# Local attention: the gate from VectorE to GpSimd, by way of a ScalarE copy, and the next group's rounded keys and queries from ScalarE to GpSimd

## The reference

```python
def windowed_sink_attention(q, k, v, sink, slopes):     # 16 heads, 4 key heads, width 64
    ...                                                 # each block of 128 queries sees 3 blocks of keys
    sc = jnp.einsum('bnqkgd,bnskd->bnkgqs', qb, kb).astype(jnp.float32) * scale + bias
    sc = jnp.where(valid[None, :, None, None], sc, -jnp.inf)
    m = jnp.maximum(jnp.max(sc, axis=-1, keepdims=True), sink_l)
    p = jnp.exp(sc - m)
    denom = jnp.sum(p, axis=-1, keepdims=True) + jnp.exp(sink_l - m)
    o = jnp.einsum('bnkgqs,bnskd->bnqkgd', (p / denom).astype(v.dtype), vb)
...
    return (oc * jax.nn.silu(gc)) @ w_out
```

## Time and profile before

| what | value |
|---|---|
| median of 3 runs | 2405.64 us (2405.22 to 2407.04) |
| the profiled execution | 2409.29 us, span 2408.0 us |
| TensorE matmul busy | 96% of the span |
| VectorE, ScalarE, GpSimd busy | 58%, 47%, 39% |
| local attention in the span | from about 1055 to 1232 us |

### The profile page before, as it was taken

How to read it: one execution, slowest core, us unless ns; L and a number is a source line. 1 busy time by engine, 2 the same in 40 slices (tenths; PEclk the granted TensorE clock), 3 DMA queues, 4 the chain that set the end, 5 groups by cost and what they waited for, 6 DMA issues and landing times.

```text
span 2408.0 us, 31494 instructions
## 1 busy us (share of the span) xinstructions
PE 2321.7 (96%) x12074; PEld 1925.0 (80%) x12074; DVE 1395.4 (58%) x1899; ACT 1133.0 (47%) x1796; POOL 929.6 (39%) x711
## 2 busy tenths in 40 slices
PE   5999999999999999999999999999999999999998
PEld 5888789878888888876678868788877888888887
DVE  6255599768884320139973743332776666666665
ACT  5322388778883221249952474232333333333334
POOL 1111256447642212335521122112265555555551
PEclk9999999999999999999999999999999999999999
DMA  8255300010003221100031221121211111111111
GB/s 307 76 158 168 93 6 1 4 34 1 1 1 123 87 74 44 53 1 1 10 106 44 77 79 44 36 96 53 71 35 53 53 53 53 53 53 53 53 53 70
DMA packets 154091, 146.48 MB, mean 61 GB/s; under 512 B 12295, under 2 KB 141365, under 8 KB 152021
## 3 DMA queue, kind: packets, MB, share of 16 engines
q1 hardware_dynamic: 153940, 144.45, 19.3%
HBM read 123.85 MB, written 16.78 MB: 58 GB/s over the span
## 4 chain that ended last, share of the span: by engine, by line
PE 81%; ACT 6%; DVE 5%; issue 5%; POOL 2%; DMA 1%; SPq 0%; ACTq 0%; DVEq 0%; POOLq 0%
PE ps L256 36%; PE ps L2650 15%; PE ps L2667 9%; PE ps L1126 5%; PE ps L1149 4%; PE ps L1136 4%; ACT C_PR L1807 1%; PE ps L1696 1%; DMA MKW<-in_ada_w 1%; POOL WSL L2567 1%; ACT B_PR L1210 1%; PE ps L1675 1%; PE ps L2626 1%; ACT B_PTH L1204 1%; PE ps L1662 1%
## 5 line engine op out<-in xcount | busy, mean ns | idle before, releaser
L243 POOL TENSOR_TENSOR WL<-WR,WH 128x1024 fp32r<-128x1024 f32 (+2 forms) x87 | 203.6, 2341 | 766.1 <-ACT WH L238 765.9
L256 PE MATMUL ps<-HH,WH 128*128 128x512 f32 (+2 forms) x1136 | 358.8, 397 | 0.0
L256 PE MATMUL ps<-HL,WH 128*128 128x512 f32 (+2 forms) x1136 | 352.1, 391 | 0.0
L256 PE MATMUL ps<-HH,WL 128*128 128x512 f32 x1104 | 341.3, 391 | 0.0
L256 PEld LDWEIGHTS ps<-HL,WH 128*128 128x128 f32 (+2 forms) x1136 | 212.4, 187 | 47.8
L256 PEld LDWEIGHTS ps<-HH,WH 128*128 128x128 f32 (+2 forms) x1136 | 208.3, 187 | 46.7 <-issue 4.1
L256 PEld LDWEIGHTS ps<-HH,WL 128*128 128x128 f32 x1104 | 208.2, 189 | 44.0
L2880 DVE TENSOR_TENSOR XF<-ps,XF 128x1024 f32<-128x1024 f32 x168 | 201.5, 1220 | 32.7 <-PE ps L2667 26.1
L2650 PE MATMUL ps<-HC,WSH 128*128 128x512 f32 x640 | 197.0, 389 | 0.0
L1162 DVE TENSOR_REDUCE NM<-ps 128x1 f32<-128x1024 f32 x128 | 156.5, 1223 | 33.5 <-PE ps L1126 32.0
L2567 POOL TENSOR_TENSOR WSL<-WSR,WSH 128x512 fp32r<-128x512 f32 x100 | 131.5, 1315 | 107.6 <-ACT WSH L2561 107.6
(11 more groups left out here) (433 smaller groups left out, 5183.0 us busy)
## 6 DMA issues: line engine op xcount, KB each, us to landing
WS<-in_w_ffn_in SPq DMA_DIRECT2D x44, 512.0 KB, 5.0
MKW<-in_ada_w SPq DMA_DIRECT2D x32, 512.0 KB, 4.3
spill<-X SPq DMA_DIRECT2D x3, 4096.0 KB, 13.6
OW<-in_w_ffn_out SPq DMA_DIRECT2D x22, 512.0 KB, 3.5
WR<-in_odd_w_in SPq DMA_DIRECT2D x19, 512.0 KB, 4.0
WR<-in_w_in SPq DMA_DIRECT2D x19, 512.0 KB, 3.9
WR<-in_even_w_in SPq DMA_DIRECT2D x17, 512.0 KB, 4.2
AWK<-in_ada_w SPq DMA_DIRECT2D x8, 1024.0 KB, 9.4
```

The lines of the kernel that those rows point to most:

```text
L243: pool.tensor_tensor(low[:, :, :], raw[:, :, :], high[:, :, :].bitcast(F32), ALU.subtract).then_inc(*w_low.up(t))
L256: last = pe.matmul(ps[0:w.out, 2 * s + h, :], wt[:, k, :], x[:, k, halves(h)], start=(k == 0 and n == 0), stop=(k == w.kt - 1 and n == len ...
```

## The change

The gate leaves VectorE. ScalarE copies the spread inverse sums from PSUM into C_G, in the odd unit 2g + 3, and GpSimd multiplies C_G in place by the silu gates in unit 2g + 4. TensorE's spread waits for ScalarE's copy of the group before, where it waited for VectorE's gate. The rounded keys and queries of the next head group are made by GpSimd as copies into the rounded format, in the same units (5, 7 and 9) in which ScalarE made them. Those of the first head group stay with ScalarE.

```diff
@@ pe_c_spread(g)
         if g:
-            pe.wait_ge(*c_gated.at(g - 1))
+            pe.wait_ge(*c_ri_moved.at(g - 1))
@@ VectorE
-    def dve_c_gate(g):
-        i, n = g // TT, g % TT
-        dve.wait_ge(*c_spread.at(g))
-        if g >= 2:
-            dve.wait_ge(*c_mixed.at(g - 2))
-        dve.tensor_tensor(C_G[:, g % 2, :].rearrange("p (t n) -> p t n", t=2),
-                          ps[:, 7, 0:2 * P].rearrange("p (t n) -> p t n", t=2), mix_pair(i, n),
-                          ALU.mult).then_inc(*c_gated.up(g))
...
-            if u % 2 == 0 and 4 <= u < NU + 4:
-                dve_c_gate((u - 4) // 2)
@@ ScalarE
+    def act_c_move_inverse(g):
+        act.wait_ge(*c_spread.at(g))
+        if g >= 2:
+            act.wait_ge(*c_mixed.at(g - 2))
+        act.activation(C_G[:, g % 2, :], ps[:, 7, 0:2 * P], ACT.Copy).then_inc(*c_ri_moved.up(g))
...
-            i = u // 16 + 1
-            if i < C_KV:
-                if u % 16 == 5:
-                    act_c_keys(i)
-                elif u % 16 in (7, 9):
-                    act_c_query(2 * i + (u % 16 - 7) // 2)
-            elif u % 16 == 5 and u < NU:
+            if u % 2 == 1 and 3 <= u < NU + 3:
+                act_c_move_inverse((u - 3) // 2)
+            if u == 16 * (C_KV - 1) + 5:
                 act_high(ODD_OUT[0])
@@ GpSimd
+    def pool_c_next_keys(i):
+        base = (i % 2) * HD
+        for r in range(2):
+            c_pool_in_turn()
+            pool.tensor_copy(C_KH[rows(r, HD), i, :], KC[base:base + HD, i // 2, :]).then_inc(*c_next_key.up(i, r))
+
+    def pool_c_next_query(t):
+        if t >= 4:
+            pool.wait_ge(*c_scored.at(2 * (8 * (t // 2 - 2) + 7) + t % 2, 1))
+        c_pool_in_turn()
+        pool.tensor_copy(C_QH[t % 4][:, :], QC[:, t, :]).then_inc(*c_next_query.up(t))
+
+    def pool_c_gate(g):
+        i, n = g // TT, g % TT
+        pool.wait_ge(*c_ri_moved.at(g))
+        c_pool_in_turn()
+        wide = C_G[:, g % 2, :].rearrange("p (t n) -> p t n", t=2)
+        pool.tensor_tensor(wide, wide, mix_pair(i, n), ALU.mult).then_inc(*c_gated.up(g))
...
             if u % 2 == 0 and 2 <= u <= NU:
                 pool_c_wide((u - 2) // 2)
+            if u % 2 == 0 and 4 <= u < NU + 4:
+                pool_c_gate((u - 4) // 2)
             if u % 2 == 1 and 5 <= u < NU + 5:
                 pool_c_mix((u - 5) // 2)
             i = u // 16 + 1
             if i < C_KV:
                 if u % 16 in (1, 2, 3, 4):
                     pool_c_bias(i, u % 16 - 1)
+                elif u % 16 == 5:
+                    pool_c_next_keys(i)
                 elif u % 16 == 6:
                     pool_c_keys(i)
+                elif u % 16 in (7, 9):
+                    pool_c_next_query(2 * i + (u % 16 - 7) // 2)
                 elif u % 16 in (8, 10):
                     pool_c_query(2 * i + (u % 16 - 8) // 2)
```

More of the change, by code:

```diff
@@ L1540, in evict @@
                 if i == 12:
-                    act_c_keys(0)
+                    act_c_keys()
                 elif i < 15:
@@ L1625, in build @@
     c_scored, c_turned, c_spread, c_summed = signal("c_scored"), signal("c_turned"), signal("c_spread"), signal("c_summed")
[L1626 to L1629, removed]
+    c_biased, c_low, c_inverse, c_added, c_key_low0, c_query_low0, c_sinks = signal("c_dve").steps(
+        "biased", "low", "inverse", "added", "key_low0", "query_low0", "sinks")
+    c_raised, c_high, c_moved, c_ri_moved, c_key_high, c_query_high, c_sink = signal("c_act").steps(
+        "raised", "high", "moved", "ri_moved", "key_high", "query_high", "sink")
     c_pool = signal("c_pool")
-    c_mixed, c_wide, c_bias, c_v_high, c_values, c_key_low, c_query_low = c_pool.steps(
-        "mixed", "wide", "bias", "v_high", "values", "key_low", "query_low")
+    c_mixed, c_gated, c_wide, c_bias, c_v_high, c_values, c_next_key, c_next_query, c_key_low, c_query_low = c_pool.steps(
+        "mixed", "gated", "wide", "bias", "v_high", "values", "next_key", "next_query", "key_low", "query_low")
     def window(n):
@@ L1776, in dve_attention_c, with act_c_keys @@
                 dve_c_low(u - 2)
-            if u % 2 == 0 and 4 <= u < NU + 4:
-                dve_c_gate((u - 4) // 2)
             if u % 2 == 1 and 5 <= u < NU + 5:
                 dve_c_add((u - 5) // 2)
-    def act_c_keys(i):
-        base = (i % 2) * HD
+    def act_c_keys():
         for r in range(2):
-            act.activation(C_KH[rows(r, HD), i, :], KC[base:base + HD, i // 2, :], ACT.Copy).then_inc(*c_key_high.up(i, r))
+            act.activation(C_KH[rows(r, HD), 0, :], KC[0:HD, 0, :], ACT.Copy).then_inc(*c_key_high.up(0, r))
     def act_c_query(t):
[L1788 to L1791, removed]
+        act.wait_ge(*vc_turned.at(1))
         act.activation(C_QH[t % 4][:, :], QC[:, t, :], ACT.Copy).then_inc(*c_query_high.up(t))
@@ L1862, in pool_c_keys @@
         for r in range(2):
-            pool.wait_ge(*c_key_high.at(i, 1))
             c_pool_in_turn()
@@ L1866, in pool_c_keys @@
                                C_KH[base:base + HD, i, :].bitcast(F32), ALU.subtract).then_inc(*c_key_low.up(i, r))
+    def pool_c_next_keys(i):
[14 more added lines that the diff above has]
+        pool.tensor_tensor(wide, wide, mix_pair(i, n), ALU.mult).then_inc(*c_gated.up(g))
     def pool_c_query(t):
-        pool.wait_ge(*c_query_high.at(t))
         c_pool_in_turn()
```

## The result

The changed kernel takes 2414.61 us (median of 5 runs, 2412.84 to 2415.83), the kernel before 2405.22 in the same comparison (median of 5, 2399.75 to 2407.04). The ratio is 1.0045, 95% interval 1.0034 to 1.0056: slower by 0.45%, some 9 to 11 us. The forecast was 2419.3, with a range of 2404 to 2424.

What follows compares the result with a forecast made beforehand. TensorE, VectorE and ScalarE were taken to share the bound of local attention within a few per cent. Backlog +10.1 and clock +3.6 us gave +13.7 on the median 2405.64: 2419.3 us, range 2404 to 2424.

Steps and rivals of the forecast that it cites:

- likeliest case: Local attention: GpSimd's backlog plus one to three clock falls, +11.9 to +15.5 us; chance 0.45.
- rival D: Local attention: GpSimd's backlog as worked out but no fall of the clock, +10.1 us, 2415.7; chance 0.24.
- +10.1 us for the backlog: GpSimd's late widenings delay TensorE's spread in the first three head groups: +3.1, +3.5 and +3.5 us.
- what is regained is at most TensorE's idle 0.18 us in the next group: After a late spread, TensorE can recover only its 0.18 us of shown idle time per group.
- +3.6 us for the clock: TensorE's clock halves after two of three stalls of about 3.5 us, costing 1.8 us each.
- The gate is worth nothing on VectorE: Taking VectorE's 32 gate multiplies away saves 0 us, since they lie under the loop TensorE - VectorE - ScalarE.
- ScalarE's copy at no cost: ScalarE's 32 copies of the spread inverse sums out of PSUM cost 0 while the spread is on time; uncovered, 10 us.
- ScalarE's relief, 5.1 us: Losing 6 key and 6 query roundings alone gives back 1.7 us in each of three head groups.
- Rival A: VectorE bounds local attention, so removing its gate and ScalarE's roundings saves 16.6 us, 2389; chance 0.06.
- B: Rival: GpSimd's backlog is absorbed and ScalarE's relief counts, -5.1 us, 2400.5; chance 0.06.
- C: Rival: GpSimd's copies near their lower bound and no clock falls, +2.6 us, 2408; chance 0.11.
- F: Rival: GpSimd's copies at their upper bound, +16 us more, 2435, or GpSimd and VectorE hinder each other; chance 0.08.

Runs made afterwards that it cites:

- e5: The kernel before with only GpSimd's two low parts of the next keys moved from unit 6 to unit 7; ratio to before 1.0040, stage +9.4 us.
- e4: The change with the gate left on VectorE and GpSimd's key and query roundings spread one piece per unit; ratio to before 0.9974, stage 156.1 us.
- e6: The whole change, gate and roundings on GpSimd, with the roundings spread out in e4's order; ratio to before 0.9989, stage 160.1 us.
- e7: e6 with the widening placed ahead of the mix in GpSimd's list; ratio to before 0.9978, stage 156.4 us.
- e9: The change with 14 unused filler matmuls on TensorE in the long stall of each of three head groups; ratio to before 1.0024, stage 169.7 us.
- e2: The change with the gate left on VectorE, so only the key and query roundings move to GpSimd; ratio to before 1.0032, stage 166.5 us.
- e3: The kernel before with VectorE's gate cut to 4 of 128 columns of each half from the third group on; ratio to before 0.9998.
- e10: e4 with VectorE's gate cut as in e3; ratio to the kernel before 0.9978, stage 155.8 us.
- e1: The change with the next keys and queries still rounded by ScalarE, so only the gate moves; ratio to before 1.0008, stage +2.4 us.

## Why the prediction was right, point by point

The median grew by 9.4 us where 13.7 were forecast. 2414.61 lies in the stated range, but just below the 2415 to 2422 of the likeliest case and nearer to rival D (2415.7), which had no fall of the clock. The falls came all the same; the backlog was smaller than worked out. So the direction and the mechanism were right, both terms were mis-sized, and that the time lies near D's is chance.

- **Where the loss is.** The spread waits for GpSimd's widening, once for 3.5 us in each of three head groups. That was the forecast's main step, and the change's trace shows it with the length that was worked out (about 3.5; measured 3.62, 3.49, 3.49). e5 shows that the place in the list is enough, e4, e6 and e7 that the same work spread out in the list costs no more than 2.7 us of waits (e7) or 8.4 in short pieces (e6), and leaves the stage shorter than before.
- **The durations on GpSimd.** Taken from the nearest rows, they held: key copy 1036 ns, query copy of 128 partitions 1036 (forecast 1.04 for both), gate 731 to 736 (forecast as the mix, 738). The list from the first mix to the fifth widening's end took 1129.41 - 1101.30 = 28.1 us, forecast 28.75. The table groups took the 10.32 us worked out. The difference lies behind them, in the 0.16 us that I put behind every operation: ahead of the copies and the low parts it was less, 0.06 to 0.13 us, as between the mix at 1121.04 and the copy at 1121.90.
- **+10.1 us for the backlog was too much.** e9, which has no falls behind its stalls, gives it alone: 169.7 - 162.6 = 7.1 us (7.4 without the first group), 0.2 of them in the fourth head group. Two steps failed by size. In the second head group of e9 the fifth spread came 3.2 us later, counted from the first, than before, not 3.7: the list was shorter. And "what is regained is at most TensorE's idle 0.18 us in the next group" didn't hold: from that spread to the next head group's first, e9 took 19.29 us against 19.92, so 0.6 us came back over four groups. There it made two spreads 4.79 us apart where before had 5.44. Together 2.6 us, where I had 3.5. Idle time that a row shows ahead of an instruction isn't all the slack: when the other engines are ahead, the matmuls' own starts close up too.
- **+3.6 us for the clock.** Measured 3.1 (3.3 without the first group), by other parts than I put it: three falls at 0.5 to 1.8 us, not two at 1.8, since two of them were half as long. That the totals lie so close is partly luck. The granted clock after the first and the third stall was

```profile
1076.00:1080.00 4.00, 1.95 (x9) 1.18 (x10) 0.62 (x3) 0.93 (x2) 3.55 (x5) 0.74 0.01 2
1080.00:1084.00 4.00, 4.00 (x23) 3.21 (x24) 2.42 (x6) 2.60 (x6) 3.50 (x4) 0.84 0.00 0
```

```profile
1169.00:1173.00 4.00, 2.93 (x13) 2.17 (x14) 0.95 (x3) 0.67 (x2) 3.62 (x4) 0.63 0.01 4
1173.00:1177.00 4.00, 4.00 (x26) 2.95 (x26) 2.42 (x8) 3.00 (x9) 3.34 (x6) 0.94 0.01 2
```

  that is (0.26 + 0.16) x 4 / 0.5 = 3.4 us at 1.2 GHz, and 3.4 again, against 6.9 after the second by the rows of the change shown with e9. In this execution the trace is with the rule of the Trainium skill that I had weighed ("TensorE: Matmul & The Clock Gate", part 1): a fall after each of the three. The stalls of 2.5 us in e2 and e5 were followed by a fall in four of six cases, the waits of up to 1.08 us in e6 by none.
- **The gate is worth nothing on VectorE.** e3 (-0.2 us) and e10 (-0.3) confirm it, with VectorE's waits for the scores up by 6.7 us in e3.
- **ScalarE's copy at no cost.** Nearly: 378 ns each. It costs 0.3 us in the fourth head group, nearly all in the group in which ScalarE rounds a weight tile, and 2.1 us over the other three where ScalarE keeps its roundings (e1).
- **ScalarE's relief, 5.1 us.** Seen in e4: 1.7 and 1.9 us in the second and third head group, as forecast (1.7 each), and 1.6 in the first without its first group. 5.1 in all.
- **Sum.** 7.1 + 3.1 = 10.2 of the stage's 10.3 us, forecast 13.7; without the first group 7.4 + 3.3 = 10.7, all of it. Rival A is out by e3, B by the spread's waits, C by the copies' 1036 ns and by e9, D by the falls, F by the same 1036 ns. F's other part, GpSimd and VectorE hindering each other, is not seen in this stage: GpSimd's mix took 738 ns before and after, VectorE's bias 610 and 611, its low part 954 both times.

## What to carry to other kernels

An engine at half load can still be the bound. What counts is what stands in its list ahead of a small result that a full engine waits for: add up the list from the last point at which it waited, and compare it with the time at which the result is due. Relief of an engine pays only where no other loop is equally long; cut the operation to a few columns and see. Put long side work behind the urgent operation, one piece in each slot: the same work went from +0.45% (the change) to -0.22% (e7) that way.

## What the runs showed of the hardware that was not expected

- A stall of about 3.5 us in a stage that is otherwise busy brought TensorE to 1.2 GHz each time, but for 3.4 or for 6.9 us, so the same stall cost 0.5 to 0.7, 1.8 and 0.9 us beside what it held up itself. One of 2.5 us did so in four of six cases. Filling the stall with matmuls that nobody reads held the clock.
- A matmul of the 32-bit identity with itself (128x128, not rounded) is two records of the trace: 26 took 5.97 us, 0.23 us each. A transpose of the same size is one: six are six records, and took 0.88 us.
- GpSimd's rounding copy takes 1036 ns for 1024 columns, the same on 64 and on 128 partitions.
- One execution can carry a wait and a fall of the clock that the next doesn't. The wait of 2.91 us and the fall behind it are nearly all of the 6.1 us by which the changed kernel entered the stage earlier. The VectorE operation waited for took 3.27 us there and 1.29 in the profile after; why isn't shown.
